# Wider matmuls in the gated feed-forward panels, a regrouped first w_down panel and an earlier start of merge panels in a two-block transformer kernel

## The reference, cut to what matters

```python
def swiglu(x, w_gate, w_up, w_down):
    return (jax.nn.silu(x @ w_gate) * (x @ w_up)) @ w_down

for l in range(DEPTH):                                   # DEPTH = 2, D = 1024, D_FF_2 = 2816
    x = x + 0.5 * swiglu(rmsnorm(x, ffn1_norm[l]), ffn1_w_gate[l], ffn1_w_up[l], ffn1_w_down[l])
    proj = rmsnorm(x, mix_norm[l]) @ w_in[l]
    # o_a: sparse attention, o_b: gated linear attention, gm: merge gates, all from proj
    y = gm[:, :, 0] * (o_a @ w_branch_nsa[l]) + gm[:, :, 1] * (o_b @ w_branch_gla[l])
    x = x + y @ w_out[l]
    x = x + 0.5 * swiglu(rmsnorm(x, ffn2_norm[l]), ffn2_w_gate[l], ffn2_w_up[l], ffn2_w_down[l])
return rmsnorm(x, final_norm)
```

## Time and profile before

| | us |
|---|---|
| median of 3 executions | 2855.32 |
| lowest and highest | 2852.97 and 2857.37 |
| the profiled execution, its own time | 2854.13 |
| its span, first to last instruction | 2852.3 |
| around the span | 1.8 |
| PE busy in the span | 2752.6 (97%) |
| POOL busy | 1756.8 (62%) |
| ACT busy | 1248.8 (44%) |
| DVE busy | 949.0 (33%) |
| 1 MB loads of the three feed-forward weights | 132 |

### The profile page before, as it was taken

The page is one execution under the profiler, slowest core; times in us unless marked ns, Lnnn a source line. Parts: engine busy times, 40 slices in busy tenths (PEclk is TensorE's granted clock), DMA queues, the critical chain, the costliest instruction groups (busy, mean ns, idle before and its releaser), DMA issues.

```text
span 2852.3 us, 48339 instructions
## 1 busy us (share of the span) xinstructions
PE 2752.6 (97%) x19897; PEld 2436.4 (85%) x19897; DVE 949.0 (33%) x1905; ACT 1248.8 (44%) x1667; POOL 1756.8 (62%) x1336
## 2 busy tenths in 40 slices
PE   7999999999999999999999999999999999999999
PEld 5765678868888676798999999999999999989999
DVE  3144341351111544433224313354322314354330
ACT  4334542342322446544444444555444435554443
POOL 1402044434454252586987977558998987757995
PEclk8999999999999999999999999999999999999999
DMA  6554533223223245554544557435555557534553
GB/s 208 149 163 137 163 115 102 91 62 101 98 94 104 45 130 166 153 174 140 193 167 153 182 161 218 138 103 172 185 177 176 179 178 194 165 104 153 180 183 119
DMA packets 401893, 418.93 MB, mean 147 GB/s; under 512 B 78890, under 2 KB 371874, under 8 KB 401423
## 3 DMA queue, kind: packets, MB, share of 16 engines
q1 hardware_dynamic: 401712, 416.37, 47.0%
HBM read 415.27 MB, written 3.16 MB: 147 GB/s over the span
## 4 chain that ended last, share of the span: by engine, by line
PE 86%; DVE 5%; ACT 3%; DMA 2%; POOL 1%; issue 1%; SPq 1%; DVEq 0%; ACTq 0%; POOLq 0%
PE ps L931 31%; PE ps L915 23%; PE ps L899 15%; PE ps L942 15%; PE ps L959 2%; POOL ring_r L1819 1%; DMA ring<-in_w_in 1%; ACT arena L2120 1%; ACT ring_hi L1872 1%; DVE stat L2937 1%; DVE arena L2951 0%; DVE hT_r L3186 0%; SPq L583 0%; DMA ring<-in_w_branch_gla 0%; DMA ring<-in_w_ada 0%
## 5 line engine op out<-in xcount | busy, mean ns | idle before, releaser
L1819 POOL TENSOR_TENSOR ring_r<-ring,ring_hi 128x512 fp32r<-128x512 f32 x1328 | 1754.5, 1356 | 1065.3 <-ACT ring_hi L1872 1037.3
L931 PE MATMUL ps<-hT_r,ring_hi 128*128 128x256 f32 (+1 forms) x5952 | 862.9, 303 | 6.5 <-POOL ring_r L1819 2.4
L931 PEld LDWEIGHTS ps<-hT_r,ring_hi 128*128 128x128 f32 x5952 | 795.8, 190 | 61.3 <-issue 14.9
L1872 ACT ACTIVATE ring_hi<-ring 128x2048 fp32r<-128x2048 f32 x312 | 596.4, 1912 | 424.3 <-DMA ring<-in_ffn_w_down 152.1
L915 PE MATMUL ps<-arena_r,ring_hi 128*128 128x256 f32 (+1 forms) x2784 | 438.9, 303 | 6.9 <-DVE arena L3224 3.1
L942 PE MATMUL ps<-hT_r,ring_r 128*128 128x256 f32 (+1 forms) x2976 | 441.2, 301 | 0.0
L942 PEld LDWEIGHTS ps<-hT_r,ring_r 128*128 128x128 f32 x2976 | 402.1, 190 | 19.6
L915 PEld LDWEIGHTS ps<-arena_r,ring_hi 128*128 128x128 f32 x2784 | 385.8, 190 | 30.2 <-DVE arena L3224 3.9
L915 PE MATMUL ps<-arena_r,ring_r 128*128 128x256 f32 (+1 forms) x1392 | 242.4, 302 | 0.0
L915 PEld LDWEIGHTS ps<-arena_r,ring_r 128*128 128x128 f32 x1392 | 201.7, 190 | 10.3
L899 PE MATMUL ps<-arena 128*64 128x128 f32 (+9 forms) x1616 | 187.5, 343 | 9.4 <-ACT arena L2106 3.3
(11 more groups left out here) (344 smaller groups left out, 2690.4 us busy)
## 6 DMA issues: line engine op xcount, KB each, us to landing
ring<-in_w_in SPq DMA_DIRECT2D x74, 1024.0 KB
ring<-in_w SPq DMA_DIRECT2D x64, 1024.0 KB
ring<-in_w_ada SPq DMA_DIRECT2D x48, 1024.0 KB
ring<-in_ffn_w_up SPq DMA_DIRECT2D x44, 1024.0 KB
ring<-in_ffn_w_gate SPq DMA_DIRECT2D x44, 1024.0 KB
ring<-in_ffn_w_down SPq DMA_DIRECT2D x44, 1024.0 KB
ring<-in_w_in SPq DMA_DIRECT2D x48, 256.0 KB
ring<-in_w_o SPq DMA_DIRECT2D x8, 1024.0 KB
```

The lines of the kernel that those rows point to most:

```text
L931: mm = pe.matmul(o, w[0], a[x], start=j == 0 and x == 0, stop=False, skip_group_check=True)
L1819: ins = pool.tensor_tensor(k.ring_lo[s][:, part], k.ring[s][:, part], k.ring_hi[s][:, part], ALU.subtract)
L1872: act.activation(k.ring_hi[s][:, :], k.ring[s][:, :], ACT.Copy).then_inc(k.hi_ready[s], 1)
```

## The change

`high_weights` multiplies one weight tile with both activation halves in one matmul of 512 columns, so that rounded weights with the high half land in columns 0 to 255 of the bank and rounded weights with the low half in columns 256 to 511. `low_weights` adds the third pass to columns 0 to 255. `wide_halves` is the loop over panels with them, and `normed_panel(halves=True)` uses them too. The two column halves of each tile are then added: ACT copies columns 256 to 511 out of PSUM (`low_moved`), and DVE adds the copy to columns 0 to 255 in place ahead of its multiplication. On the first w_down panel the eight tiles are taken in groups of four, two and two, and banks are taken group by group, both feature tiles of the panel within a group. In the merge the nsa panels, w_branch_gla panels 1 to 3 and w_out panels 1 and 2 are taken with `late=True` by `two_results`.

```diff
+        self.h2_both = hbuf_r[:, 0:2 * KD * SEQ].rearrange("p (x k t) -> p k x t", x=2, k=KD)
...
+            def high_weights(bs, w, kt):
+                for b, m in zip(bs, range(2)):
+                    mm = pe.matmul(ps[:, b, :].rearrange("p (x t) -> p x t", x=2), w[0][:, kt, m * P:m * P + P], k.h2_both[:, kt],
+                                   start=kt == 0, stop=False, skip_group_check=True)
...
+            def low_weights(bs, w, kt):
+                return [pe.matmul(ps[:, b, 0:SEQ], w[1][:, kt, m * P:m * P + P], h2[0][:, kt, :], start=False,
+                                  stop=kt == KD - 1, skip_group_check=True) for b, m in zip(bs, range(2))]
+            def wide_halves(panels):
+                for _ in range(panels):
+                    w = view(panel(late=True), 0, KD, 256)
+                    bs = [bank() for _ in range(2)]
+                    for kt in range(KD):
+                        high_weights(bs, w, kt)
+                    s, low_of[0] = low_of[0], None
+                    pe.wait_ge(k.lo_ready[s], T.split_rounds(s))
+                    for kt in range(KD):
+                        mms = low_weights(bs, w, kt)
+                    for b, mm in zip(bs, mms):
+                        mm.then_inc(k.bank_done[b], 1)
...
             def ffn():
-                normed_panel(h2)
-                wide(1)
+                normed_panel(h2, halves=True)
+                wide_halves(1)
                 with pe.Fori(0, 5) as i, T.loop(i, 5, {"panel": 4, "tiles": 8}):
-                    wide(4)
+                    wide_halves(4)
...
                     if kt == 0:
-                        bs = [bank() for _ in range(KD)]
-                    if kt < FT - 2:
+                        bs = []
+                        for tiles in (range(4), range(4, 6), range(6, KD)):
+                            bs += [bank() for _ in tiles]
+                            for j in range(2):
+                                abreast([ps[:, bs[m], 0:SEQ] for m in tiles], ...
+                    elif 1 < kt < FT - 2:
...
             def merge():
-                    w = view(panel(), 0, 4, 512)
+                    w = view(panel(late=True), 0, 4, 512)
...
+                        if j in (1, 2) or sem == "ob_split" and j == 3:
+                            w = view(panel(late=True), 0, KD, 256)
+                            two_results(SEQ, [tile(w, m, x_split, ALL) for m in range(2)])
+                            continue
...
+                    def low_moved(m, b, v):
+                        act.wait_ge(k.bank_done[b], v)
+                        act.activation(low[:, m, :], ps[:, b, SEQ:2 * SEQ], ACT.Copy).then_inc(S["low_moved"], 1)
...
                         for m, (b, v) in enumerate(tiles):
-                            dve.wait_ge(k.bank_done[b], v)
+                            dve.wait_ge(S["low_moved"], T.next("low_moved"))
+                            ins = dve.tensor_tensor(ps[:, b, 0:SEQ], ps[:, b, 0:SEQ], low[:, 2 * g + m, :], ALU.add)
+                        ins.then_inc(S["tiles_summed"], 1)
+                        dve.wait_ge(S["tiles_summed"], T.next("tiles_summed"))
```

More of the change, by code:

```diff
@@ L418 @@
 HID, HID_HI, HID_SLOTS = 0, 4 * KD * TOK, 4
-A2, A2_HI, SILU2, PLAIN2, SQ2, STD2 = 0, 5632, 11264, 12288, 16400, 18448
+A2, A2_HI, SILU2, PLAIN2, LOW2, SQ2, STD2 = 0, 5632, 11264, 12288, 14336, 16400, 18448
 (QA, KSLC, KWIN, VSLC, VWIN, GA, KCMP, VCMP, HIDK, ALR, PCT, OA, PROB2, PROBT2, QB, KB, KIN, Z, T1, VB,
@@ L1502, in normed_panel @@
                     pe.wait_ge(S["h_ready"], T.next("h_ready"))
-                    mms = abreast([ps[:, b, 0:SEQ] for b in bs],
-                                  [tile(w, m, x, ALL)[kt:kt + 1] for m in range(2)], kt == 0, kt == KD - 1)
+                    if halves:
+                        high_weights(bs, w, kt)
+                        mms = low_weights(bs, w, kt)
+                    else:
+                        mms = abreast([ps[:, b, 0:SEQ] for b in bs],
+                                      [tile(w, m, x, ALL)[kt:kt + 1] for m in range(2)], kt == 0, kt == KD - 1)
                     if kt == KD // 2:
@@ L1767, in merge @@
                         for kt in range(KD):
-                            if j == 0 and kt % tiles == 0:
+                            if kt % tiles == 0:
                                 pe.wait_ge(S[sem], T.next(sem))
@@ L2333, in pair @@
                 def pair(j, two, first=False):
+                    low = area(LOW2, 2, 4, SEQ)[:, j % 2]
+                    def low_moved(m, b, v):
+                        act.wait_ge(k.bank_done[b], v)
+                        act.activation(low[:, m, :], ps[:, b, SEQ:2 * SEQ], ACT.Copy).then_inc(S["low_moved"], 1)
                     if first:
                         strips_moved()
-                    split()
-                    skip(2)
+                        split()
+                    up = [T.take() for _ in range(2)]
                     if first:
                         deviation()
+                    for m in range(2):
+                        low_moved(m, *up[m])
                     split()
-                    skip(2)
-                    if first:
-                        split()
+                    for m in range(2, 4):
+                        low_moved(m, *T.take())
+                    split()
                     s = area(SILU2, 2, 2, SEQ)[:, j % 2]
@@ L3231, in ffn @@
                 pair(0, slice(0, 2), first=True)
-                with dve.Fori(0, 5) as i, T.loop(i, 5, {"tiles": 8, "silu_ready": 2, "act2_rounded": 2}):
+                with dve.Fori(0, 5) as i, T.loop(i, 5, {"tiles": 8, "silu_ready": 2, "act2_rounded": 2, "low_moved": 8,
+                                                         "tiles_summed": 4}):
                     for j in range(2):
```

18 lines of the change are left out of this document (13 added, 5 removed).

## The result

The changed kernel takes 2837.65 us (median of 4 runs, 2835.73 to 2839.17) against 2854.70 us in runs beside it: a ratio of 0.9939, 95% interval 0.9922 to 0.9956, or 17 us less (12.6 to 22.3). On a second chip, with more runs of both, it was 2833.39 against 2857.15 us: 0.9922, interval 0.9909 to 0.9936, 22 us less by that ratio (18 to 26; the two medians lie 24 apart). The forecast was 2833 us, from a sum of 22.2 us, with 2827 to 2846 us for 8 times in 10. The profiled execution took 2837.88 us, its span is 2836.1 us.

The account below looks back on a forecast made before the run. PE was taken to bound the feed-forward loop, narrowly ahead of POOL, and POOL the merge. The terms 17.9 + 0.4 + 3.5 + 0.4 = 22.2 us gave 2833 us, with 2827 to 2846 us for 8 in 10.

Parts of the forecast that it names:

- 512 columns: Up and gate panels: each merged pair saves 13.3 ns, 17.9 us over 84 wide panels, plus 0.4 us in four normed panels.
- The rival that the operand's second run costs something: Wide panels: the second run costs what merging saves, 2851 us, chance 0.10; half that cost, 2842 us, 0.03.
- The rule of the Trainium skill: Matmul time N / 2.4 + 2.5 ns: merging two saves 2.5 ns, 3.5 us for 1408 pairs, some 2848 us.
- The new work hides: Feed-forward loop: new copies on ACT and additions on DVE cost nothing; POOL keeps 1.5 to 2.1 us of reserve before w_down.
- First w_down panel: PE's 0.89 us wait for DVE's reads of the last banks, four times, goes with tile groups: 3.5 us.
- part 1: The merging into 512-column matmuls in the up and gate panels, 17.9 us, with 0.4 us for the normed panels.
- part 2: The grouping of tiles in the first w_down panel of each stage, 3.5 us.
- Merge, 0.4 us: Beginning on rounded weights takes waits out of the gla panels, but POOL is the limit: 0.4 us for both merges.
- The wait ahead of w_out: Merge: PE reaches w_out panel 0 at about 1955.1 and waits 1.7 us for POOL's low weights.
- The half clock: Rival: a clock fall may come or go in attention or at the norms, 2828 or 2838 us, chance 0.10.
- Sum: Whole kernel: 17.9 + 0.4 + 3.5 + 0.4 = 22.2 us less, new median 2833 us.

Follow-up runs that it names:

- m_flat: The changed kernel with the wide panels' 512-column operand as one unbroken run in place of two runs of 256; 2839.75 us in its one run.
- d_noadd: The changed kernel with DVE's additions cut to one column, the copies on ACT kept; 2839.7 us in its one run.
- p2_down: The kernel before with only the first w_down panel taken in groups of tiles; 2856.2 us, 0.9998.
- p1_wide: The kernel before with only the 512-column products of the up and gate panels, with their copies and additions; 2847.2 us, 0.9965.
- b_merge: The changed kernel with w_out panel 0 also begun on rounded weights, its low weights behind; 2837.56 against 2853.54 us, 0.9951.
- p3_merge: The kernel before with only the merge's panels begun on rounded weights; 2857.9 us, 1.0004.

## Why the prediction was right, point by point

- **512 columns, 17.9 + 0.4 us.** The mechanism held, the size was a little high: 5.76 - 5.57 = 0.19 us a panel, 84 x 0.19 = 16.0 us. The rival that the operand's second run costs something is excluded by m_flat. The rule of the Trainium skill (TensorE: Matmul & The Clock Gate, section Back-to-back issue gap) that stands under that rival gives 2.5 ns a merged pair and is stated there for an isolated matmul; in this stream it is 12 ns.
- **The new work hides.** Right, though not free: POOL was taken to stay at 5.39 to 5.42 us a panel and keeps 5.45 against PE's 5.57, and has the low weights of the first w_down panel at 2100.65 us, by the end of its 84th instruction of the stage, 1.4 us before PE gets to w_down at 2102.01; 1.5 to 2.1 were forecast. That the additions don't slow POOL is shown by d_noadd.
- **First w_down panel, 3.5 us.** The right wait, and its price in the kernel before: 3.8 us at equal clock, 1.05 us by a w_down part that the attention part follows (64.56 to 63.51 us in p2_down). In plain time p2_down gained nothing at its lower clock. The step that fell short is that the parts were priced one by one. The text had the last banks free 2.2 us behind the gate panel, and did not carry it over to what part 1 would cost without part 2: four waits of 2.0 us (p1_wide). The joint sum was not touched by that, since the groups cover either wait.
- **Merge, 0.4 us.** Right in size (0.19 us a merge) and in its reason: b_merge shows that behind POOL there is DVE. The wait ahead of w_out was 0.6 and not 1.7 us because POOL began sooner, after a load that landed 1.2 us sooner; where the load landed late, in p3_merge, it was 1.85 us. These 2.4 us were not in the sum. The packet of the instruction queue that no longer falls into the load is the cause that the traces point to, not one that a run has isolated.
- **The half clock, 0.10, "some 5 us to either side".** This rival came true beside the forecast on the first chip: attention took 5.9 us more, three falls more at 1.7 us each make 5.1 of them. On the second chip its profiled execution had one fall fewer there, and the time was 2833.4 us, the forecast itself; the kernel before took 2857.15 us there and not 2855.32, so the gain was above the forecast and the time met it by chance. A price of about 2 us for 0.001 of mean clock is now measured.
- **Sum.** In the profiled executions: 16.0 for the panels, 5.4 for w_down (the 21.4 us of the stages less 16.0), 2.8 in the merges, less 5.9 in attention and 2.1 ahead of the second block, which is the 16.2 us between the spans. At equal clock the change is worth 22 to 23 us and 22.2 were forecast, but 2.3 too much for the 512 columns was made up by 1.9 too little for w_down and by 2.4 from the load. These add up to 24.2 us before the clock, 1 to 2 more than the medians at equal clock give. So the mechanism of the sum held, and that its total came so close is in part luck: the errors of its terms lie either way and nearly cancel.

## What to carry to other kernels

Price the parts of a change together as well as singly: copies and additions that hide inside a loop lengthen the wait where the loop ends, and a regrouping there, worth 4 us alone, was worth 8 us behind them, and more where the clock fell behind the wait. Before a difference of a few microseconds is explained, compare the mean granted clock of the runs: here 0.001 of it is 2 us, enough to hide a gain of 3.5 us entirely. If every run of the changed kernel has the lower clock, that is part of what the change does. When a load is ready later or sooner than in another kernel, look at what else the DMA queues carry at that moment, the instruction queue too. When a wait is taken away by putting work of another kind ahead, look for what that work used to cover.

## What the runs showed of the hardware that was not expected

- Products of 64 rows and 15 columns put singly between products of 128 rows and 256 columns cost 0.16 us at every change between them: 0.63 us a round where 0.31 was the sum.
- A DVE operation of 128x256 with both inputs in SBUF takes 1233 ns beside a busy POOL (412 ns at the least), one with an input in PSUM 421 ns; POOL loses 0.20 us to each of the first and nothing to the second.
- A moving operand of 512 columns in two runs of 256 costs the same as in one, 3.65 us for sixteen. Sixteen merged pairs save 3.84 - 3.65 = 0.19 us, 12 ns each.
- With the gap ahead of a clock fall filled, that fall was gone, and the next one was 6.8 us long in place of 3.4.
- The same 1 MB load was ready 4.7 to 5.1 us after its issue in the kernels with part 1 and after 5.9 to 6.2 us in those without. In the latter, and only there, a 16 KB packet of the instruction queue fell into it, and only its last tenth came later.
